# Routing of a token tile cut from four heads and four to two, two and four, with the row gathers begun after the first two

## What is computed

```python
q = (xb @ peer_wq).reshape(128, 8, 2, 128)               # 8 heads, two halves
s = einsum('thpd,phkd->thpk', q, peer_subkeys)           # 128 keys for each half
s1, i1 = top_k(s[:, :, 0], 16); s2, i2 = top_k(s[:, :, 1], 16)
cand = s1[..., :, None] + s2[..., None, :]               # 16 x 16 for each head
sc, j = top_k(cand, 16)                                  # 16 experts for each head
eid = take(i1 * 128 + i2, j); g = softmax(sc)
a = gelu(einsum('td,thkd->thk', xb, peer_u[eid]))
y = einsum('thk,thkd->td', g * a, peer_v[eid])
```

## Time and profile before

| | |
|---|---|
| time, median of 3 runs | 2567.91 us (2565.3 to 2570.94) |
| profiled execution: span from the first to the last instruction | 2572.8 us |
| DVE busy | 1757.6 us, 68% of the span |
| PE busy | 1280.7 us, 50% |
| moved by DMA | 944.49 MB, mean 367 GB/s |

### The profile page before, as it was taken

How to read it: one execution, slowest core, us unless ns; L and a number is a source line. 1 busy time by engine, 2 the same in 40 slices (tenths; PEclk the granted TensorE clock), 3 DMA queues, 4 the chain that set the end, 5 groups by cost and what they waited for, 6 DMA issues and landing times.

```text
span 2572.8 us, 17754 instructions
## 1 busy us (share of the span) xinstructions
PE 1280.7 (50%) x6315; PEld 697.2 (27%) x6317; DVE 1757.6 (68%) x2243; ACT 212.5 (8%) x559; POOL 1184.3 (46%) x686
## 2 busy tenths in 40 slices
PE   5699998897490543266884972000015655200000
PEld 2363534482240432143331960000002222000000
DVE  1010112217967977897557667999999998899898
ACT  3110012100001221121001010000000000000000
POOL 1000100002426744575222415678876767788684
PEclk9799898899795655556995985555556677655555
DMA  9949899659999999999998989999999999999897
GB/s 299 332 172 422 324 414 291 208 196 360 388 422 397 377 366 341 405 410 370 344 373 321 414 318 410 366 393 422 422 407 407 400 420 417 417 422 422 366 422 307
DMA packets 163042, 944.49 MB, mean 367 GB/s; under 512 B 34635, under 2 KB 44435, under 8 KB 56830
## 3 DMA queue, kind: packets, MB, share of 16 engines
q0 software_dynamic: 94784, 682.66, 66.0%
q1 hardware_dynamic: 68175, 260.74, 28.2%
HBM read 937.36 MB, written 10.26 MB: 368 GB/s over the span
## 4 chain that ended last, share of the span: by engine, by line
PE 27%; DMA 25%; DVE 20%; POOL 15%; issue 9%; SPq 2%; ACT 1%; POOLq 0%; another core or an unknown queue 0%; DVEq 0%; ACTq 0%
POOL arena L668 11%; DMA arena<-in_peer_u,arena 10%; DMA arena<-in_peer_v,arena 9%; DVE arena L1975 8%; POOL arena L680 4%; DVE arena L1998 4%; DMA arena<-in_w_out 4%; PE PS L1468 3%; PE PS L1445 3%; PE PS L1016 3%; DMA arena<-in_w_ada 3%; PE PS L1166 2%; PE PS L1253 2%; PE PS L966 2%; PE PS L1423 2%
## 5 line engine op out<-in xcount | busy, mean ns | idle before, releaser
L668 POOL DMA_INDIRECT arena<-in_peer_u,arena x256 | 471.7, 1843 | 446.1 <-DVE arena L1975 240.8
L1975 DVE CUSTOM_DVE_ANT_0 arena<-arena 128x2048 f32<-128x2048 f32 x256 | 581.5, 2289 | 118.0 <-DMA arena<-in_peer_u,arena 116.7
L1998 DVE SCALAR_TENSOR_TENSOR arena<-arena 128x2048 f32<-128x2048 f32 x226 | 531.1, 2350 | 136.6 <-DMA arena<-in_peer_v,arena 131.9
L668 POOL DMA_INDIRECT arena<-in_peer_v,arena x256 | 428.3, 1673 | 369.7 <-DVE arena L1998 242.7
L1468 PE MATMUL PS<-arena 128*128 128x512 f32 x240 | 180.3, 921 | 449.9 <-DMA arena<-in_peer_v,arena 449.9
L1468 PEld LDWEIGHTS PS<-arena 128*128 128x128 f32 x240 | 69.5, 304 | 561.4 <-issue 555.1
L1474 PE MATMUL PS<-arena 128*64 128x512 f32 x8 | 5.5, 849 | 346.4 <-DVEq L2041 346.4
L2031 DVE SCALAR_TENSOR_TENSOR arena<-arena 128x2048 f32<-128x2048 f32 x64 | 150.6, 2352 | 10.8 <-DMA arena<-in_peer_v,arena 5.3
L966 PE MATMUL PS<-arena 128*32 128x512 f32 x768 | 119.4, 721 | 69.9 <-DMA arena<-in_w_ada 66.6
L2028 DVE CUSTOM_DVE_ANT_0 arena<-arena 128x2048 f32<-128x2048 f32 x64 | 145.0, 2291 | 8.4 <-DMA arena<-in_peer_u,arena 6.5
L680 POOL DMA_INDIRECT arena<-in_peer_v,arena x64 | 126.4, 1975 | 39.0 <-issue 18.6
(11 more groups left out here) (347 smaller groups left out, 1824.5 us busy)
## 6 DMA issues: line engine op xcount, KB each, us to landing
arena<-in_w_ada SPq DMA_DIRECT2D x96, 1024.0 KB, 12.1
arena<-in_w_in SPq DMA_DIRECT2D x32, 1048.0 KB, 9.2
arena<-in_peer_wq SPq DMA_DIRECT2D x32, 1024.0 KB, 10.2
arena<-in_w_in SPq DMA_DIRECT2D x32, 768.0 KB, 11.2
arena<-in_w_out SPq DMA_DIRECT2D x16, 1024.0 KB, 30.0
arena<-in_w_out SPq DMA_DIRECT2D x32, 512.0 KB, 24.0
arena<-in_peer_u,arena POOLq DMA_INDIRECT x320, 13.9
arena<-in_peer_v,arena POOLq DMA_INDIRECT x320, 15.5
```

Source lines behind the costliest of these rows:

```text
L668: pool.indirect_dma_start(out=rows_ring[:, k % NROW, :], out_offset=None, in_=tables[kind], in_offset=bass.IndirectOffsetOnAxis(ap=ids[:, ...
L1975: V.tensor_tensor_reduce(out=buf, in0=buf, in1=h2(t), scale=1.0, scalar=0.0, op0=ALU.mult, op1=ALU.add, accum_out=dots[:, t, r:r + 1]).the ...
L1998: V.scalar_tensor_tensor(out=acc[t], in0=rows_ring[:, k % NROW, :], scalar=dots[:, t, r:r + 1], in1=acc[t], op0=ALU.mult, op1=ALU.add).the ...
```

## The change

`experts` takes a first head and a number of heads. Tile 0 is routed in three parts: heads 0 and 1 alone, heads 2 and 3 beside the rows, heads 4 to 7 after them beside the rows. The waits on POOL, SP, ACT and DVE are renumbered. Tiles 1 and 2 keep their two parts of four heads. By the yields of `top16` the part of two heads has 12 steps, so all that stands behind the routing in `beside_dots` comes 12 rows later, and its steps are 124.

```diff
@@ sync
-            sp.wait_ge(s_eid, 2)
+            sp.wait_ge(s_eid, 3)
             sp.dma_start(biasP.rearrange("p a b -> p (a b)"), I["k_bias"]).then_inc(s_bp, 16)
@@ gpsimd
-                    if kind == "u" and r % 64 == 0:
-                        pool.wait_ge(s_eid, 2 * t + r // 64 + 1)
+                    if kind == "u" and r in ((0, 32, 64) if t == 0 else (0, 64)):
+                        pool.wait_ge(s_eid, r // 32 + 1 if t == 0 else 4 + r // 64)
@@ scalar
             def expert_exp(t):
-                for half in range(2):
-                    w = gw[:, t, half * HH:(half + 1) * HH]
-                    act.wait_ge(s_e2, 2 * t + half + 1)
+                parts = [(0, 2), (2, 4), (4, 8)] if t == 0 else [(0, 4), (4, 8)]
+                for i, (lo, hi) in enumerate(parts):
+                    w = gw[:, t, lo:hi]
+                    act.wait_ge(s_e2, i + 1 if t == 0 else 2 * t + i + 2)
                     A(w, w, exp).then_inc(s_e2x, 1)
@@ vector
-            def experts(t, half):
+            def experts(t, h0, nh):
...
                 if group == 0:
-                    dve.wait_ge(s_sc, 2 + 2 * half)
+                    dve.wait_ge(s_sc, (h0 + nh) // 2)
...
-                yield from top16([sc[:, 2 * HH * half + i, :] for i in range(2 * HH)], val1, idx1, 2 * HH)
+                yield from top16([sc[:, 2 * h0 + i, :] for i in range(2 * nh)], val1, idx1, 2 * nh)
...
-                yield from top16([cand[:, h].rearrange("p a b -> p (a b)") for h in range(HH)], val2, idx2, HH)
+                yield from top16([cand[:, h].rearrange("p a b -> p (a b)") for h in range(nh)], val2, idx2, nh)
...
-            for _ in experts(0, 0):
+            for _ in experts(0, 0, 2):
                 pass
...
             def beside_dots():
-                yield from experts(0, 1)
+                yield from experts(0, 2, 2)
+                yield from experts(0, HH, HH)
                 yield from pause(Q_PAUSE)
```

More of the change, by code:

```diff
@@ L938, in _ @@
             expert_exp(2)
-            act.wait_ge(s_eid, 5)
+            act.wait_ge(s_eid, 6)
             for ph, (kind, t) in list(enumerate(PHASES))[N_INLINE:]:
@@ L1745, in top16 @@
                         link(last)
-            def experts(t, half):
+            def experts(t, h0, nh):
                 group = 0 if t == 0 else 1
-                heads = slice(half * HH, (half + 1) * HH)
+                heads = slice(h0, h0 + nh)
                 b = scratch_of(group)
-                sc, cand, onehot, picked, ab_i, ab_f = b["sc"][:, GROUPS[group].index(t)], b["cand"], b["onehot"], b["picked"], b["ab_i"], b["ab_f"]
-                val1, idx1, idx1f, val2, idx2 = b["val1"], b["idx1"], b["idx1f"], b["val2"], b["idx2"]
+                sc, cand, onehot = b["sc"][:, GROUPS[group].index(t)], b["cand"][:, 0:nh], b["onehot"][:, 0:nh]
+                picked, ab_i, ab_f = [b[name][:, :, 0:nh] for name in ("picked", "ab_i", "ab_f")]
+                val1, idx1, idx1f = [b[name][:, 0:2 * nh] for name in ("val1", "idx1", "idx1f")]
+                val2, idx2 = b["val2"][:, 0:nh], b["idx2"][:, 0:nh]
                 if group == 0:
-                    dve.wait_ge(s_sc, 2 + 2 * half)
+                    dve.wait_ge(s_sc, (h0 + nh) // 2)
                 else:
                     dve.wait_ge(s_sc, 4 + 8)
-                yield from top16([sc[:, 2 * HH * half + i, :] for i in range(2 * HH)], val1, idx1, 2 * HH)
+                yield from top16([sc[:, 2 * h0 + i, :] for i in range(2 * nh)], val1, idx1, 2 * nh)
                 link(V.tensor_copy(idx1f, idx1))
@@ L1761, in experts @@
                 i1 = idx1f.rearrange("p (h two) k -> p h two k", two=2)
-                shape = [128, HH, TOPK, TOPK]
+                shape = [128, nh, TOPK, TOPK]
                 link(V.tensor_tensor(cand, v1[:, :, 0, :].unsqueeze(3).to_broadcast(shape), v1[:, :, 1, :].unsqueeze(2).to_broadcast(shape), ALU.add))
                 yield
-                yield from top16([cand[:, h].rearrange("p a b -> p (a b)") for h in range(HH)], val2, idx2, HH)
+                yield from top16([cand[:, h].rearrange("p a b -> p (a b)") for h in range(nh)], val2, idx2, nh)
                 V.tensor_scalar(ab_i[:, 0], idx2, 4, None, ALU.logical_shift_right)
@@ L1769, in experts @@
                 link(V.tensor_copy(ab_f, ab_i))
-                V.tensor_tensor(gw[:, t, heads], val2, val2[:, :, 0:1].to_broadcast([128, HH, TOPK]), ALU.subtract).then_inc(s_e2, 1)
+                V.tensor_tensor(gw[:, t, heads], val2, val2[:, :, 0:1].to_broadcast([128, nh, TOPK]), ALU.subtract).then_inc(s_e2, 1)
                 for key in range(2):
@@ L1785, in shares @@
                 w, total = gw[:, t], stat[:, 16:16 + PH]
-                dve.wait_ge(s_e2x, 2 * t + 2)
+                dve.wait_ge(s_e2x, 2 * t + 3)
                 link(V.tensor_reduce(total, w, X_AXIS, ALU.add))
@@ L1934, in beside_sums @@
                 yield from pause(WQ_PAUSE)
-                yield from experts(1, 0)
+                yield from experts(1, 0 * HH, HH)
             def beside_dots1():
-                yield from paced(experts(1, 1), 2)
+                yield from paced(experts(1, 1 * HH, HH), 2)
                 yield from pause(2)
@@ L1948, in beside_sums1 @@
                 for half in range(2):
-                    yield from paced(experts(2, half), 2)
+                    yield from paced(experts(2, half * HH, HH), 2)
                 yield from pause(2)
```

## The result

The changed kernel takes 2575.76 us, median of 8 runs (2572.79 to 2581.06), against 2570.21 us for the kernel before in the same comparison. The ratio is 1.0026, 95% interval 1.0015 to 1.0037: **slower by 0.26%**, about 6.7 us by the ratio (the two medians are 5.6 us apart). The time lies in the range of the prediction (2558 to 2580), but not in its likeliest case: 2568 us and no change had 0.47, slower had 0.25. Every ratio here is of fast runs alone; one slow run, 3155.40 us in `split_gated`, is left out of them.

A forecast was written before the change was run, and what follows sets the result against it. The limit was taken to alternate between DMA and DVE, so the sum counted bytes: 2572.8 - 6.7 + 7.2 = 2573.3 us of span, less 4.9 to the runs' scale, 2568 us; range 2558 to 2580.

The forecast's parts named there:

- likeliest case: Whole kernel: 6.7 us of transfer time gained, 7.2 us lost, so 2568 us and no change; chance 0.47.
- The earlier start: Tile 0's routing before the rows: ends 13.7 us earlier, first dot at 589.0, worth 6.7 us of transfer time.
- The late exponential: Tile 0's last routing exponential on ACT: moves from row 16 to row 28, 29 us later, and ib with it.
- its cost in bytes: DMA before ib: ring full at 680, then 33% of 22 us lacking until 702, 7.2 us lost.
- The extra DVE work: Three routing parts in place of two: some 1.1 us of overheads, hidden beside rows waiting for gathers, counted as nothing.
- the later steps: Tile 1's attention beside rows 74 to 123: 18.3 us of waits move from last dots into sums, counted as nothing.
- Rival (d): Sums: biasS has 15.1 us to land; if it takes 28.9, DVE stalls 13.8 us, 2582 us; chance 0.09.
- rival (c): Rows before ib: ring full sooner, DMA lacks 22% from 645 to 680 too, 8.2 us slower, 2576 us; chance 0.13.
- before each place where dots wait only bytes count: Rule for the sum: DVE's earlier work is settled where dots wait, so gains count in bytes not moved.
- (a): DVE decides after all: the DMA catches up somewhere and all 13.7 us stay, 2554.2 us; chance 0.10.
- (b): The late ib costs nothing, so the gained 6.7 us stay, 2561.2 us; chance 0.18.
- (e): Steps beside the rows hold up POOL's gathers: 12 added steps at 1.81 us, 21.7 us, 2590 us; chance 0.03.

The follow-up runs named there:

- split_gated: Changed kernel with heads 0, 1 and heads 2, 3 both routed alone before the rows, POOL's first gather held until the second part is done; ratio 1.0022.
- split_alone: Changed kernel with both parts of two heads routed alone before the rows, POOL free to gather after the first part; ratio to the kernel before 0.9957.
- q0_act: Changed kernel with the pause before the query norm 0 rows, not 12, and tile 0's last exponential behind the five ia copies on ACT; ratio 0.9977.
- q0: Changed kernel with the pause before the query norm set from 12 rows to 0; ratio to the kernel before 0.9977.
- before_q24: Kernel before the change with the pause before the query norm set from 12 rows to 24; ratio 1.0031.
- wout_late: Changed kernel with the first two w_out pieces (four 512 KB transfers) put behind the sample's loop on SP; ratio to the kernel before 1.0001.
- q0_wout_late: Changed kernel with the pause before the query norm 0 rows and the first two w_out pieces behind the sample's loop; ratio to the kernel before 0.9954.

## Why the prediction was right where it was, and where it failed

**The earlier start** was right: 13.7 us forecast, 14.0 measured for the first dot. Two small errors cancel in it. A part of two heads takes 15.8 us and not 15.1 (564.85 to 580.66 here, and two parts take 31.8 us in `split_alone`, 564.02 to 595.80), so the routing ends 13.0 us earlier. And the first dot waits 6.3 us for its row in place of 7.3.

**The late exponential and its cost in bytes** were right in mechanism: 28.9 us against 29, PE's wait 73.3 against 75, the ring full near 675 against 680. Counted as time times one less the busy share, the DMA's idle time from 76 to 156 us relative grew from 2.4 to 6.0 us, 3.6 where 7.2 were forecast, and in the 32 us after the zero it fell from 17.3 to 12.8, 4.5 where 6.7 were forecast. Over the 626 us from the zero the idle times are equal, 30.8 us before and 31.2 after. So both terms were too large, but "gain and loss of bytes cancel" held. With pause 0 the late `ib` was no brake, as `q0_act` shows; with pause 12 that is open.

One reading of the rows was off, with no weight in the sum: the two slices at 208 and 196 GB/s end at 579 us, and a slice at 360 lies between them and the one that begins at 643.

**The extra DVE work** was hidden beside the rows, as said, and costs when it is not (`split_gated`).

**The step that failed** is the one on the later steps: that the attention of tile 1 twelve rows later moves the sample's loads into the sums "and this term is nothing either way". I treated it as bytes that are waited for in one place or the other. That part held in kind: the MEMSET came 11.8 us earlier, and row waits of 6.9 us came back in the sums. What I left out is the time between the release of these loads and PE's need of them. For unit 0's values it shrank from 70.8 us to 38.2, and the product had to wait. PE's order then held the next scores, and those held DVE and its sum rows for 9.1 us. 11.8 less 6.9 and 9.1 is a lag of 4.2 us, and the last product is 4.3 us later. Rival (d) had the right place, and its 15.1 us for `biasS` were met exactly, but it named the wrong load: `biasS` landed in 10.9 us and no unit waited for it; the pages behind it were late.

That the time fell into the range all the same, and beside the 2576 us of rival (c), is luck: the term that lost had been put at nothing, and what (c) describes did not happen.

**A step that was missing** is what follows the sample's attention. Since DVE waits for tile 1's scores, 17.96 us in the kernel before, the rows are not what sets the end in this stretch. The argument that "before each place where dots wait only bytes count" left out that chain. With it, a lead of the rows gains only as far as it reaches the sample's last product (4.0 us of 4.1 in `q0`, nothing of 11.8 in the changed kernel), and a lag there is paid for the most part: 13.5 us become 10.2 at tile 1's MAX8 in `before_q24`, 4.3 become 3.3 in the changed kernel.

Of the rivals, (a), the kept 13.7 us, and (b), 6.7 us faster, are out for the change as made. (b) is about what `q0` shows: 5.9 us. (c) did not come: throughput held until 675. (e) would have shown before row 12 as a lead that shrinks; row 12's dot comes at 79.8 relative, where the rows' own pace had put it at about 80. And in `split_alone` POOL's first six gathers run beside the routing of heads 2 and 3 and take 0.94 to 1.02 us each, so the routing's steps did not hold POOL up, which (e) and the 2590 us beside it needed.

## What to carry to other kernels

When other work is paced by steps beside a loop, count what a change does to the place of everything behind it: a step moved by twelve rows also moves the loads that it releases, and the time until they are needed. Ask what a load that is not needed yet does to the others: here four transfers of 512 KB, issued 168 us before the projection that uses them began, held the DMA at some 290 GB/s for 20 us. Before a gain at the start is counted, find the next place where the bound engine waits for a chain, and ask whether the gain reaches that chain. If a first part of the indices is known early, let the gathers start on it even if the arithmetic does not: here one wait of the issuing engine, released earlier, was worth 0.65%, and the arithmetic's order stayed as it was.

## What was not expected of the hardware

The DMA can be fully busy and yet move 29% less. At a busy share of 1.02 it moved 293 GB/s from 1012 to 1032 us in the kernel before, 294 from 1040 to 1060 in the changed kernel and 291 from 1005 to 1025 in `q0`. In `wout_late` and `q0_wout_late`, which issue the four `w_out` transfers later, the windows of the same times have 413 and 414 GB/s, with gathers and, in the first, cache pages going on. Each of the four writes to 64 of the 128 partitions; whether that is the reason, or their shape in memory, no run here shows.
